# One core, two stacked models: the row statistics of every norm kept one per token, the memory's low part in two halves, and the scan's order of work

## What is computed

```python
def rmsnorm(x, g):
    xf = x.astype(jnp.float32)
    y = xf * lax.rsqrt(jnp.mean(xf * xf, axis=-1, keepdims=True) + EPS)
    return (y * g.astype(jnp.float32)).astype(x.dtype)

# attn_layer: by head, 64 channels
qa = rmsnorm(heads(qa, H_A), q_norm_a)
ka = rmsnorm(heads(ka, H_A), k_norm_a)
# ssm_layer: by group, 512 channels
y = y.reshape(b, s, D_INNER) * jax.nn.silu(z.astype(jnp.float32))
yg = y.reshape(b, s, SSM_GROUPS, D_INNER // SSM_GROUPS)
yg = yg * lax.rsqrt(jnp.mean(yg * yg, axis=-1, keepdims=True) + EPS)
```

## Time and profile before

| | us |
|---|---|
| median of three runs | 2999.2 (2995.01 to 3000.9) |
| the profiled execution, its own time | 2994.11 |
| its span on the core | 2992.3 |
| TensorE (PE) busy | 2871.9, 96% |
| VectorE (DVE) busy | 1934.2, 65% |
| ScalarE (ACT) busy | 1427.9, 48% |
| GpSimd (POOL) busy | 1326.8, 44% |
| granted TensorE clock, mean over the span | 0.989 |

### The profile page before, as it was taken

One profiled execution on the slowest core, in us unless ns is written; L12 is line 12 of the kernel. 1 busy time (PEld: TensorE's weight loads), 2 busy tenths in 40 slices (PEclk: granted clock), 3 DMA queues, 4 the chain that ended last, 5 costly groups with the idle time before them and its releaser, 6 DMA issues.

```text
span 2992.3 us, 45754 instructions
## 1 busy us (share of the span) xinstructions
PE 2871.9 (96%) x16254; PEld 2384.1 (80%) x16254; DVE 1934.2 (65%) x2984; ACT 1427.9 (48%) x2534; POOL 1326.8 (44%) x710
## 2 busy tenths in 40 slices
PE   7999999999998999999998999999999999999998
PEld 4667789988875688989767878898877778788986
DVE  4445958665617648658698438594788853495856
ACT  4555535454356435445555435353544443353534
POOL 3323444444456434444588424454542343244543
PEclk9999999999999999999999999999999999999999
DMA  4112222322220122323213213233322232232322
GB/s 151 40 33 82 90 95 91 113 92 91 92 85 1 50 95 82 113 92 101 97 65 127 85 43 106 92 109 100 103 93 65 75 100 73 61 106 99 100 100 84
DMA packets 77323, 259.58 MB, mean 87 GB/s; under 512 B 9408, under 2 KB 9536, under 8 KB 76736
## 3 DMA queue, kind: packets, MB, share of 16 engines
q1 hardware_dynamic: 74320, 249.42, 25.3%
q10 hardware_dynamic: 2160, 4.86, 0.5%
q0 software_dynamic: 640, 2.62, 0.3%
HBM read 253.71 MB, written 2.10 MB: 85 GB/s over the span
## 4 chain that ended last, share of the span: by engine, by line
PE 67%; DVE 19%; issue 5%; ACT 4%; DMA 3%; POOL 2%; DVEq 0%; ACTq 0%; SPq 0%; POOLq 0%
PE bank L930 9%; PE bank L932 9%; PE bank L931 9%; PE bank L1683 5%; PE bank L1684 5%; PE bank L1685 5%; DVE t_raw L2525 2%; DVE t_lo L2532 2%; PE bank L1103 1%; PE bank L1104 1%; PE bank L1105 1%; PE bank L1654 1%; PE bank L1655 1%; PE bank L1656 1%; PE bank L1150 1%
## 5 line engine op out<-in xcount | busy, mean ns | idle before, releaser
L751 POOL TENSOR_TENSOR w_lo<-w_raw,w_hi 128x1024 fp32r<-128x1024 f32 (+2 forms) x273 | 595.3, 2184 | 881.9 <-ACT w_hi L2719 881.8
L2719 ACT ACTIVATE w_hi<-w_raw 128x1024 fp32r<-128x1024 f32 (+2 forms) x427 | 423.0, 992 | 415.5 <-DMA w_raw<-w_pw 49.4
L887 POOL TENSOR_TENSOR w_lo<-w_raw,w_hi 128x512 fp32r<-128x512 f32 x216 | 353.4, 1640 | 433.0 <-DVE t_raw L2525 433.0
L721 POOL TENSOR_TENSOR w_lo<-w_raw,w_hi 128x1024 fp32r<-128x1024 f32 x82 | 200.8, 2451 | 255.0 <-ACT w_hi L2719 255.0
L2532 DVE TENSOR_TENSOR t_lo<-t_raw,t_hi 128x512 fp32r<-128x512 f32 x288 | 251.9, 899 | 6.7 <-DVE t_raw L2525 0.5
L930 PE MATMUL bank<-xh,w_hi 128*128 128x512 f32 x584 | 234.3, 401 | 0.9 <-DVE xl L1745 0.6
L931 PE MATMUL bank<-xl,w_hi 128*128 128x512 f32 x584 | 230.4, 395 | 0.0
L932 PE MATMUL bank<-xh,w_lo 128*128 128x512 f32 x584 | 230.4, 395 | 0.0
L930 PE MATMUL bank<-hh,w_hi 128*128 128x512 f32 x528 | 210.2, 398 | 4.1 <-POOL w_lo L751 4.1
L931 PE MATMUL bank<-hl,w_hi 128*128 128x512 f32 x528 | 210.1, 398 | 0.0
L932 PE MATMUL bank<-hh,w_lo 128*128 128x512 f32 x528 | 210.0, 398 | 0.0
(11 more groups left out here) (429 smaller groups left out, 8347.7 us busy)
## 6 DMA issues: line engine op xcount, KB each, us to landing
w_raw<-w_ssm_in SPq DMA_DIRECT2D x41, 512.0 KB, 3.4
w_raw<-w_pw SPq DMA_DIRECT2D x24, 512.0 KB, 3.5
w_raw<-w_diff_in SPq DMA_DIRECT2D x24, 512.0 KB, 3.5
w_raw<-w_attn_in SPq DMA_DIRECT2D x18, 512.0 KB, 3.6
...
```

The lines of the kernel that those rows point to most:

```text
L721: pool.tensor_tensor(w_lo[:, slot, :], w_raw[:, slot, :], w_hi[:, slot, :].bitcast(F32), ALU.subtract).then_inc(w_split, 1)
L751: pool.tensor_tensor(w_lo[:, slot, 0:n], w_raw[:, slot, 0:n], w_hi[:, slot, 0:n].bitcast(F32), ALU.subtract).then_inc(w_split, 1)
L887: ins = pool.tensor_tensor(w_lo[:, s % SLOTS, cs], w_raw[:, s % SLOTS, cs], w_hi[:, s % SLOTS, cs].bitcast(F32), ALU.subtract)
L2719: act.activation(w_hi[:, slot, 0:n], w_raw[:, slot, 0:n], ACT.Copy).then_inc(w_half, 1)
```

## The change

1. **Statistics by token.** In every norm `acc` (or the squares) becomes the weights of four small products, one per block of 128 tokens, with one column of ones; the sums then stand as 128 tokens by 4 columns. Root and reciprocal work on 128x4. Four products of the column, broadcast to 128 columns as weights, with the identity (`norm_spread`, `spread_group`) spread it back to 128x512 in PSUM, and VectorE copies a stage norm's to `rstd`. TensorE makes the spread two products-of-three-products after the sum. Head norms: per chunk four products with two columns of the picking matrix, and eight spreads of 64 output partitions; the reciprocal is one of 128x16 or 128x8. The matrix `heads` and its making are gone.
2. **Final norm.** It multiplies out of PSUM without a copy; the rounded part and rest of the last residual (`xh`, `xl`) are not made any more.
3. **Memory's low** in two instructions of 128x1024, two weight slabs apart.
4. **Scan.** The first step's shares are made three weight slabs earlier on GpSimd; state 2 stands before the decays on VectorE; half of the lows stand some steps later.

```diff
@@ class of helper functions
+        def head_cols(i, t):
+            return slice(2 * (NT * i + t), 2 * (NT * i + t) + 2)
+        def low_at(n):
+            if n % NT == 0 or n > KI and n % NT != 3:
+                return normed_at(n - 1)
+            return normed_at(n - 3) if n % NT == 3 and n < KI else ()
@@ GpSimd
-            def memory_lower():
-                memories[0] += 1
-                pool.wait_ge(m_half, memories[0])
-                pool.tensor_tensor(m_lo[:], m_in[:], m_hi[:].bitcast(F32), ALU.subtract).then_inc(m_split, 1)
+            def memory_lower(o):
+                if o in (LEAD, LEAD + 2):
+                    ks = slice(0, KD // 2) if o == LEAD else slice(KD // 2, KD)
+                    pool.wait_ge(m_half, memories[0])
+                    pool.tensor_tensor(m_lo[:, ks, :], m_in[:, ks, :], m_hi[:, ks, :].bitcast(F32), ALU.subtract).then_inc(m_split, 1)
...
                 if c == 41:
                     ssm_decay(0, 1)
                     ssm_decay(0, 2)
+                    ssm_shares(0)
@@ TensorE, attention
                 def sums(g):
                     for i, c in enumerate(GROUPS[g]):
                         pe.wait_ge(q_sq, NORMED.index(c) + 1)
-                        pe.matmul(bank[7][0:32, :], pick[:, 30 - 2 * i:62 - 2 * i], sq[:, i, :], start=(i == 0),
-                                  stop=(c == GROUPS[g][-1]), skip_group_check=True).then_inc(q_sum, 1)
+                        for t in range(NT):
+                            mm = pe.matmul(bank[7][:, head_cols(i, t)], sq[:, i, t * P:(t + 1) * P], pick[:, 30:32],
+                                           start=True, stop=True, skip_group_check=True)
+                        mm.then_inc(q_sum, 1)
                 def spread(c):
                     g, i = place_of(c)
-                    pe.wait_ge(q_rec, 2 * g + 2)
-                    pe.matmul(bank[7][:], heads[:, i * P:(i + 1) * P], acc[0:32, :], start=True, stop=True).then_inc(q_bc, 1)
+                    pe.wait_ge(q_rec, g + 1)
+                    for t in range(NT):
+                        for half in range(2):
+                            n = head_cols(i, t).start + half
+                            mm = pe.matmul(bank[7][64 * half:64 * half + 64, t * P:(t + 1) * P], acc[:, n:n + 1].broadcast_to([P, 64]),
+                                           ident[:], start=True, stop=True, skip_group_check=True)
+                    mm.then_inc(q_bc, 1)
@@ TensorE, scan
+                def spread_group(g):
+                    pe.wait_ge(s_rec, g + 1)
+                    for t in range(NT):
+                        n = NT * g + t
+                        mm = pe.matmul(spread_bank(g)[:, of(t)], s_r[:, n:n + 1].broadcast_to([P, P]), ident[:],
+                                       start=True, stop=True, skip_group_check=True)
+                    mm.then_inc(s_sum, 1)
...
+                    if n >= NT + 3 and n % NT == 3 and n < KI:
+                        spread_group(n // NT - 1)
@@ TensorE, stage norms
                 pe.wait_ge(x_acc, KD * nrm[0])
-                pe.matmul(NORM_BANK[:], ones[:], acc[:], start=True, stop=True).then_inc(nrm_sum, 1)
+                for t in range(NT):
+                    mm = pe.matmul(NORM_BANK[:, t:t + 1], acc[:, t * P:(t + 1) * P], ones[:, 0:1], start=True, stop=True,
+                                   skip_group_check=True)
+                mm.then_inc(nrm_sum, 1)
+            def norm_spread():
+                pe.wait_ge(nrm_ready, 2 * nrm[0] - 1)
+                for t in range(NT):
+                    mm = pe.matmul(NORM_BANK[:, t * P:(t + 1) * P], rstd[:, t:t + 1].broadcast_to([P, P]), ident[:],
+                                   start=True, stop=True, skip_group_check=True)
+                mm.then_inc(nrm_sum, 1)
@@ VectorE
-                dve.reciprocal(rstd[:], root).then_inc(nrm_ready, 1)
-                dve.wait_ge(nrm_ready, nrm[0])
+                dve.reciprocal(rstd[:, 0:NT], rstd[:, 0:NT]).then_inc(nrm_ready, 1)
+                dve.wait_ge(nrm_sum, 2 * nrm[0])
+                dve.tensor_copy(rstd[:], NORM_BANK[:]).then_inc(nrm_ready, 1)
...
+                    if (n // NT, 8) in items:
+                        state(n // NT, 2)
                     if n < KI:
                         decays(2 * n)
                         decays(2 * n + 1)
-                    if (n // NT, 8) in items:
-                        state(n // NT, 2)
...
-                    for f in normed_at(n - 1):
+                    for f in low_at(n):
                         low(f)
...
-                def inverse(g, part):
+                def inverse(g):
                     dve.wait_ge(q_root, g + 1)
-                    r = acc[0:32, part * 256:(part + 1) * 256]
+                    r = acc[:, 0:2 * NT * len(GROUPS[g])]
                     dve.reciprocal(r, r).then_inc(q_rec, 1)
@@ ScalarE
-                act.activation(root, NORM_BANK[:], ACT.Sqrt, scale=1.0 / D, bias=eps[:, 0:1]).then_inc(nrm_root, 1)
+                act.activation(rstd[:, 0:NT], NORM_BANK[:, 0:NT], ACT.Sqrt, scale=1.0 / D, bias=eps[:, 0:1]).then_inc(nrm_root, 1)
```

141 lines of the change are left out of this document (91 added, 50 removed).

## The result

| | before | after |
|---|---|---|
| median of the runs, us | 2999.6 (2995.01 to 3000.9, four runs) | 2967.5 (2962.68 to 2974.72, four runs) |
| the profiled execution, its own time | 2994.11 | 2962.68 |
| its span | 2992.3 | 2960.9 |
| TensorE idle between products, us | 108.2 | 83.6 |
| mean granted clock | 0.989 | 0.995 |

The ratio is 0.9898, with a 95% interval of 0.9874 to 0.9921: 32 us faster, where 35 were forecast (2964, range 2948 to 2981). Later the changed kernel ran again: 2964.2 (2962.5 to 2967.17, five runs), ratio 0.9895 (0.9876 to 0.9913). The median of all nine runs is 2964.8. The four runs above went with their clock: 2962.7 us at 0.995, 2965.7 at 0.993, 2969.3 at 0.991, 2974.7 at 0.989. What follows leans on stages and steps, which repeat far better than the whole.

The account below looks back on a forecast made before the run. TensorE, busy 2871.9 of 2992.3 us, was taken as the bound, with its waits and half-clock stretches to gain. Terms 3.6 - 4.2 - 14.6 - 7.5 - 10.1 - 2.3 = -35.1 gave 2964 us, range 2948 to 2981.

Parts of the forecast that it names:

- Feed forwards, -4.2: Four feed forwards' stage norms: VectorE's 1.0 us lead counts, not TensorE's 0.9; -1.0 each, -4.2 us with the tenths.
- Attention, SSM and memory attentions, +0.9 each: Stage norms where TensorE is full: the added spread counts in full, +0.9 us in each of four stages, +3.6.
- Differential attention, 0: Its stage norm: TensorE waits for GpSimd and VectorE by more than the spread's cost, so 0 us change.
- Attention, -14.6: Attention's head norms: five reciprocal waits go, -7.4 us; slow clock stretches go, -6; cheaper head spreads, -1.2.
- The memory's low, -7.5: GpSimd's low in halves: both TensorE waits behind it go, -4.1 us, and slow clock stretches behind them, -3.4.
- The scan, -10.1: SSM scan: shares -2.6, state -3.6, VectorE time -4.5, four spreads +3.6, clock -3; sum -10.1 us.
- Much of this VectorE time was not waited for; I take -4.5: Scan: three 3.35 us reciprocals and stretched lows leave VectorE's order; -4.5 us, bounds -2 and -8.
- State before decays: -3.6: Scan: state placed before the decays on VectorE removes 3.6 of TensorE's 4.2 us wait for a state.
- The end, -2.3: Final norm: first final multiplication about 4.4 us after the sum's start, not 6.2; -2.3 us including 0.5 from earlier squares.
- Waits handed on: Rival: other operations become late instead, half of attention's and the scan's waits remain; -5.8 us, 2993; chance 0.06.
- Halves not side by side: Rival: head spread's output halves run in line, near 0.11 us per record; 2974 us; chance 0.08.
- Weight loads in the open: Rival: 568 records' own TensorE weight loads are not hidden, costing 85 us; 3049 us; chance 0.03.

Follow-up runs that it names:

- the second execution: A second profiled execution of the changed kernel, nothing altered, from its later repeat against the kernel before; 2964.2 us median, ratio 0.9895.
- h_serial: Changed kernel with each head spread's products run lower 64 output partitions first, then upper 64, instead of alternating; 2974.1 us, ratio 0.9935 to the kernel before.

## Why the prediction was right

The time came within 3.5 us of the forecast (2967.5 for 2964; nine runs, 2964.8), for the most part by the mechanisms named, with one term too large and two too small. That the scan's shortfall and the gains of attention and the end nearly cancel is luck. Point by point:

- **Prices.** The spread 0.9 (measured 0.8 to 0.9), the sum by token 0.9 (0.8), `rstd` after 4.1 (4.07), the head spread 0.96 (1.02): all held. The root and reciprocal of 128x4, taken at 0.2 each from nothing better, are 0.26 and 0.18.
- **Feed forwards, -4.2.** Held: the old form costs 4.5 in them. What counts is VectorE's lead.
- **Attention, SSM and memory attentions, +0.9 each.** Held in the memory attentions (127.6 to 128.5 and 128.6). In the other two it can't be told from scatter.
- **Differential attention, 0.** Too low: the stage is 322.2 before and 323.2 to 324.9 in eight executions with the new form. The step "TensorE waits in them for GpSimd and VectorE by more than this" took waits later in the stage for a cover. They are none: at the norm itself the products run on, so the spread's 0.8 is in full, and here TensorE does wait for `rstd` (0.43 to 0.44 us, in all eight and in none with the old form), since VectorE stands in a 1.4 us pair of `ol` when the root is ready (2149.97) and comes to the reciprocal 0.83 later, as the timeline of the kernel after has it:

```profile
2149.47 1.41 DVE L2092 SCALAR_TENSOR_TENSOR ol<-xt,cols,oh 128x512 fp32r<-128x512 f32 x2
...
2150.80 0.17 DVE L1846 RECIPROCAL rstd<-rstd 128x4 f32<-128x4 f32 x1
...
2151.02 1.16 PE L1697 MATMUL bank<-ident,rstd 128*128 128x128 f32 x8 [0.44 <-DVE rstd L1846]
```

  These are 1.2. The changed kernel with the old form put back has 320.3 to 320.6 in five executions, some 3 less, but the kernel before, with the same form, 322.2. The difference of those two lies in TensorE's waits for ScalarE's probabilities (4.95 us before, 3.7 to 3.9 in the five; 3.7 to 6.6 with the new form) and for VectorE's `a_pt_t` (3.2 before, 2.2 to 2.3 in the five). So the rest of the 3 is in waits that also differ where the form does not, and what sets them stays open.
- **Attention, -14.6.** The right mechanism, and undone alone it costs 15.6 in the stage. The clock part was 5.1 there, against 6 taken, and from before to after 17.0 us of half clock became 3.4, up to 6.8; the spreads gave 0.4 at most (13 by 0.03), against 1.2.
- **The memory's low, -7.5.** Held: undoing it costs 6.4 in one execution, with one of the two stretches of half clock.
- **The scan, -10.1.** The term that failed: 6.5 (122.3 to 115.8, from the first decays' product to the first output product). The three terms for waits, -2.6, -3.6 and -4.5, were 10.7 together; TensorE's idle time in steps 1 to 15 fell by 6.9 (19.3 to 12.5). Inside it, "Much of this VectorE time was not waited for; I take -4.5" was still too much: the lows gave 1.1 of waits, in one step, and the reciprocals less than the spreads took. And "State before decays: -3.6" gave 2.1, since the squares behind it became the late ones, a wait that no part of the prediction named. The shares' wait gave its 2.6. The clock's -3 can't be judged by one execution: half clock in these steps went from 13.1 us to 6.8, and in the second execution to 13.7.
- **The end, -2.3.** 3.3 in one execution and 1.7 in the other, by clock.
- **The rivals.** "Waits handed on" (2993) happened in one place, the scan's squares, at 1.28 us three times (twice in the second execution), not as a rule. "Halves not side by side" (2974) is what h_serial shows it would have looked like, at 0.09 a record and not 0.11. Weight loads in the open: TensorE has 484 more records and 2.7 us less busy time. Less half clock is part of that, but up to 13.6 us of it hide no 85, so no. The lows that would be stretched again wherever they meet GpSimd meet it no more: none of the sixteen begins while a GpSimd instruction runs, and all take 0.68 to 0.69.

Of the marks under "what would show it", two failed by their size: the scan's idle time was to be under 12 us and is 15.9 (14.2 in the second execution), and the products of sums wait 4.4 us less for `p_two` over the four feed forwards, and with their other waits (21.8 to 16.0 in all) 5.8 less, 1.5 a stage and not 2.
